# Semaphores of a stage left behind are cleared before, not after, the ring fills of the stage that runs

## The reference, cut to what matters

```python
x = _layer_norm(DEEPNORM_ALPHA * x + h, ln1_g[layer], ln1_b[layer])
x = _layer_norm(DEEPNORM_ALPHA * x + _sq_relu_mlp(x, mlp_w1[layer], mlp_w2[layer]), ...)
...
x = x + jnp.einsum('bsd,de->bse', y, w_out[l])
h = rmsnorm(x, norm_ffn_g[l])
gu = jnp.einsum('bsd,df->bsf', h, w_ffn_in[l])
x = x + jnp.einsum('bsf,fd->bsd', jax.nn.silu(g_ff) * u_ff, w_ffn_out[l])
```

## Time and profile before

| what | value |
|---|---|
| median of 3 runs | 3461.35 us (3458.49 to 3462.01) |
| time of the profiled execution | 3461.23 us |
| its span, first to last instruction | 3459.4 us |
| TensorE (PE) busy | 3207.1 us, 93% |
| VectorE (DVE) busy | 1867.3 us, 54% |
| ScalarE (ACT) busy | 1162.3 us, 34% |
| GpSimd (POOL) busy | 153.7 us, 4% |
| mean granted clock of TensorE | 0.967 |

### The profile page before, as it was taken

One profiled execution on the slowest core, in us unless ns is written; L12 is line 12 of the kernel. 1 busy time (PEld: TensorE's weight loads), 2 busy tenths in 40 slices (PEclk: granted clock), 3 DMA queues, 4 the chain that ended last, 5 costly groups with the idle time before them and its releaser, 6 DMA issues.

```text
span 3459.4 us, 41500 instructions
## 1 busy us (share of the span) xinstructions
PE 3207.1 (93%) x16984; PEld 2490.1 (72%) x16984; DVE 1867.3 (54%) x2802; ACT 1162.3 (34%) x1805; POOL 153.7 (4%) x129
## 2 busy tenths in 40 slices
PE   9968879999899978999989899999999989999999
PEld 6648757787677756887666578788877747878887
DVE  4673454243567755333376664664647665466463
ACT  4332234132333334322254232432334323243232
POOL 0122200000000000000100000100000000010000
PEclk9979989999999989999999999999999999999999
DMA  4110012222211112222311112223222112222322
GB/s 168 61 49 3 19 49 86 83 88 86 78 64 61 66 34 73 97 98 86 118 49 61 49 67 92 98 88 101 90 77 97 61 49 73 98 88 86 102 91 79
DMA packets 41560, 264.84 MB, mean 77 GB/s; under 512 B 4600, under 2 KB 4984, under 8 KB 13980
## 3 DMA queue, kind: packets, MB, share of 16 engines
q1 hardware_dynamic: 41364, 262.18, 22.1%
q10 hardware_dynamic: 8, 0.01, 0.0%
HBM read 260.07 MB, written 3.42 MB: 76 GB/s over the span
## 4 chain that ended last, share of the span: by engine, by line
PE 73%; DVE 8%; ACT 3%; issue 2%; SPq 0%; DVEq 0%; ACTq 0%
PE psum L338 21%; PE psum L339 21%; PE psum L340 21%; DVE w_lo L320 1%; PE psum L763 1%; PE psum L910 1%; ACT tiles L940 1%; PE psum L919 1%; PE psum L1844 1%; PE psum L1845 1%; PE psum L1846 1%; PE psum L1756 1%; DVE tiles L965 1%; DVE tiles L1648 1%; ACT xT L794 1%
## 5 line engine op out<-in xcount | busy, mean ns | idle before, releaser
L338 PE MATMUL psum<-hi,w_hi 128*128 128x512 f32 x3672 | 1478.8, 403 | 77.0 <-SPq L433 28.2
L339 PE MATMUL psum<-lo,w_hi 128*128 128x512 f32 x3672 | 1459.4, 397 | 0.0
L340 PE MATMUL psum<-hi,w_lo 128*128 128x512 f32 x3672 | 1458.6, 397 | 0.0
L338 PEld LDWEIGHTS psum<-hi,w_hi 128*128 128x128 f32 x3672 | 694.9, 189 | 261.6 <-issue 72.6
L320 DVE TENSOR_TENSOR w_lo<-ring,w_hi 128x1024 fp32r<-128x1024 f32 (+1 forms) x495 | 604.4, 1221 | 466.9 <-ACT w_hi L312 466.3
L312 ACT ACTIVATE w_hi<-ring 128x1024 fp32r<-128x1024 f32 (+1 forms) x495 | 505.1, 1021 | 978.4 <-PE psum L340 917.8
L339 PEld LDWEIGHTS psum<-lo,w_hi 128*128 128x128 f32 x3672 | 695.0, 189 | 169.2 <-issue 5.3
L340 PEld LDWEIGHTS psum<-hi,w_lo 128*128 128x128 f32 x3672 | 693.8, 189 | 170.4
L728 DVE SCALAR_TENSOR_TENSOR xT<-xT,psum 128x512 f32<-128x512 f32 x96 | 66.0, 687 | 240.2 <-PE psum L340 240.2
L940 ACT ACTIVATE tiles<-tiles,small 128x256 f32<-128x256 f32 (+3 forms) x176 | 95.0, 541 | 167.6 <-DVE small L965 167.0
L1524 DVE TENSOR_TENSOR tiles<-tiles 128x512 f32<-128x512 f32 x64 | 44.3, 693 | 180.6 <-ACT tiles L1516 180.6
(11 more groups left out here) (238 smaller groups left out, 2542.6 us busy)
## 6 DMA issues: line engine op xcount, KB each, us to landing
ring<-in_weights SPq DMA_DIRECT2D x211, 1024.0 KB, 4.8
ring<-in_weights SPq DMA_DIRECT2D x28, 704.0 KB, 4.0
ring<-in_weights SPq DMA_DIRECT2D x4, 896.0 KB, 4.5
ring<-in_weights SPq DMA_DIRECT2D x3, 832.0 KB, 4.3
xT<-in_x SPq DMA_DIRECT2D x8, 256.0 KB, 6.0
tiles<-bias_repeated SPq DMA_DIRECT2D x8, 256.0 KB, 5.3
out<-xT SPq DMA_DIRECT2D x8, 256.0 KB, 2.1
held<-in_const SPq DMA_DIRECT2D x1, 1344.0 KB, 5.8
```

What stands on the lines that cost most here:

```text
L338: pe.matmul(out, hi, rhs.hi(first + at), start=(at == 0), stop=False)
L339: pe.matmul(out, hi, rhs.lo(first + at), start=False, stop=False)
L340: last = pe.matmul(out, lo, rhs.hi(first + at), start=False, stop=(at == total - 1))
```

## The change

The clear of a stage moves ahead of the fills of the rest of the stage; the fill ahead of it now reaches three units (`AHEAD`) further than the end of the lead. Nothing is added or removed, and PE, DVE, ACT and POOL have the same instructions in the same order.

```diff
             for st in stages:
                 if st.lead_end is not None:
-                    k.fill(sp, st.lead_end)
+                    k.fill(sp, st.lead_end + AHEAD)
                 if st.loads is not None:
                     st.loads(sp)
+                st.clear(k, sp)
                 if st.end is not None:
                     k.fill(sp, st.end + AHEAD)
-                st.clear(k, sp)
                 if st.stores is not None:
                     st.stores(sp)
```

## The result

The changed kernel takes **3402.75 us** (median of 4 runs, 3402.52 to 3403.99), against 3461.68 us of the kernel before on the same chip. The ratio is 0.9831, 95% interval 0.9814 to 0.9848. A second set of five runs gave 3401.47 us and 0.9833 (0.9820 to 0.9847). The forecast was 3405 us, range 3396 to 3421.

What follows compares the result with a forecast made beforehand. TensorE, busy 3207 of 3459.4 us, was taken to set the time through its work, idle time and low-clock time. 40.4 + 6.8 + 10.5 − 1 = 56.7 us off 3461.2 gave 3405 us, range 3396 to 3421.

Steps and rivals of the forecast that it cites:

- The waits: TensorE's six waits on the clear, at borders 4/5 to 9/10, would go: 28.2 + 12.2 = 40.4 us removed.
- The clock at the product borders: Behind the four product borders, 15.0 us of half-clock busy time would run at full clock, saving 6.8 us.
- The clock at the attention borders: Behind the two attention borders, 22.8 us of half-clock busy time would run at full clock, saving at most 10.5 us.
- The rival next in chance: Waits go, but retention behind the attention borders keeps the low clock, so 10.5 us stay: 3415 us, chance 0.20.
- Fills behind the clear: On SP's queue, fills held behind the early clear (3.2 to 4.2 us) have 21 us of slack: cost 0.
- The start: 74 clears ahead of fill 3 delay it about 4.2 us, but DMA engines are busy anyway: 0, at most 4.2 us.
- The loads of stage 9: Bias loads start some 4 us later behind two extra fills: cost between 0 and 2 us, taken as 1 us.
- the shift covered: In stage 7, a layer norm between the loads and the first product was to cover the same shift of the loads.
- the three terms: The gains at the six borders: waits 40.4 us, clock behind product borders 6.8 us, clock behind attention borders 10.5 us.
- The 1.5 us that I allowed: A single border's low clock could end one step sooner or later, some 1.5 us each, giving the forecast 3396 to 3411.

Runs made afterwards that it cites:

- counting late: Changed kernel with the clears still early, but the one count of `cleared` that lets engines into the next stage left behind the stage's last fill: 3445.53 us.
- held eight times over: Changed kernel with the clears of stages 5 to 10 made eight times over, holding the fills behind them: 3407.34 us, one run.

## Why the prediction was right

- **The waits, 40.4 us.** Right, and gone from every engine's waits. The chain of the earlier trace rows had named the mechanism, and counting late confirmed its two parts, 24 us of clears and 16.6 us of place. Nothing took their place: the windows inside stage 6 were the right thing to read for what is late next.
- **The clock at the product borders, 6.8 us.** The four gained 35.8 us together, and 28.2 + 6.8 is 35.0. The run with only the attention borders free put the same work at 35.5 us.
- **The clock at the attention borders, 10.5 us.** The least certain term. The two gained 23.4 us, and 12.2 + 10.5 is 22.7. It holds because the clock stays at 1.00 from the first retention matmul on. The rival next in chance, that the retention starts at half clock even without the gap, is out by that, though the stated range held its time too. That a shorter gap can keep the clock down there for 24 us, as the late count showed, the prediction did not see.
- **Fills behind the clear, 0.** Right, and the room is what its terms give: 21 us for a late fill and some 11 us until the next one is due are 32 us, and held eight times over, ScalarE first waited after about 32 us. The rule of the Trainium skill, page "DMA: Bandwidth & Descriptors", section "Rules for kernel authors", to issue transfers early did not bear here: clears made four times over left the time where it was (3402.92 us).
- **The start, 0 (at most 4.2).** Fill 3 was issued at us 15.13 instead of 10.71. ScalarE's waits for transfers were 8.0 instead of 6.6 us, and with this clear put back the time was the same within 0.2 us.
- **The loads of stage 9, 1 us.** Wrong in place, and open in size. VectorE did wait 2.4 us for the bias in stage 9, but TensorE lost nothing by it. What reached TensorE was in stage 7, where I had called the shift covered: there the late bias meets the layer norm on VectorE, which is worth 0.3 to 0.4 us. It is the second half of the edit, the three units more ahead of the loads, that costs this, and it brings nothing. The medians put that half at 2.6 and 4.7 us, above the 2 us that I had allowed; most of this no trace ties to it.

The forecast was 2 us above the measured time. So small a distance is partly luck: the borders gained 59.2 us, 1.5 more than the three terms, and elsewhere 2.0 us were lost instead of 1. In the recurrent stages alone, the low clock differs by 2 us of busy time between traces of kernels that are the same there. The 1.5 us that I allowed for a low clock that ends one step sooner or later stands in no row ahead of the prediction. Shifts of 1.5 and 1.6 us did turn up, but away from the borders.

The best version measured is the one with the clear alone moved, 3398.05 and 3398.84 us, 0.1% below the changed kernel.

## What to carry to other kernels

Bookkeeping such as clearing semaphores should go where its condition becomes true, not at the end of the section that it belongs to. On a queue whose last transfer of a section waits for the compute engines, whatever is put behind it starts late by construction. When a gap of TensorE is priced, the matmuls behind it must be read for their clock: here gaps of 6 to 8 us cost another quarter of their length behind products (6.8 of 28.2 us), and almost as much as themselves behind small matmuls (10.5 of 12.2 us). Before trusting that a wait is replaced by nothing, look for the same passage elsewhere in the trace without the wait.

## What was not expected of the hardware

- Three gaps of 3.5 us of TensorE at product borders were followed by half clock just as those of 6 to 8 us were; one of 2.6 us was not. Where gaps of 1.7 to 3.5 us were left, the same program took 3433.7 us in one execution and 3445 to 3446 us in three others.
- Once down, the clock stayed at half for 24 us of gapless retention matmuls in one execution, while in another place and in other kernels the same matmuls ran at full clock from the start.
- A GpSimd addition on 128x128 tiles took 0.45 us on its own and beside VectorE's reciprocal, and 0.90 us beside VectorE's multiplications, of which the first two took 0.86 and 0.94 us instead of 0.68 us.
